# Mixing stage: output norm in the next step's first slots, decay scans behind the third low product, another spread of the logits

## What is computed

```python
def rwkv7_time_mix(z, shift0, wkv0, mu, w0, w2, a0, a2, g2, k_k, k_a, r_k, lnx_g, lnx_b):
    zm = zf + (prev - zf) * mu                      # r, k, v, xw, xa, xg are columns of zm
    wlog = -softplus(-(w0 + tanh(xw) @ w2)) - 0.5
    decay = exp(-exp(wlog))
    a = sigmoid(a0 + xa @ a2)
    g = sigmoid(xg) @ g2
    kk = heads(k * k_k);  kk = kk * rsqrt(max(sum(kk * kk), 1e-24))
    k = k * (1.0 + (a - 1.0) * k_a)
    # per row: s = s * w + (s @ -kk) (kk * a)^T + v k^T;  y = s @ r
    y, s_new = wkv7_scan(rh, heads(decay), kh, vh, -kk, kk * ah, wkv0)
    y = (y - mean) * rsqrt(var + LN_X_EPS)          # the output norm, per head
    y = y.reshape(B, L, RWKV_DIM) * lnx_g + lnx_b
    bonus = sum(rh * kh * r_k) * vh
    return (y + bonus) * g, s_new, z[:, -1:]
# in layer_forward, of the same projection p = h @ w_in:
    gate_logits = p[..., MLA_COLS + RWKV_COLS:]     # 2048 columns
    x = x + sum(sigmoid(gate_logits) * proj)
```

## Time and profile before

| | us |
|---|---|
| median of the timed runs (3) | 1544.85 |
| lowest, highest | 1543.92, 1545.82 |
| the profiled execution | 1542.08 |
| its span, first to last instruction | 1540.3 |
| PE busy in the span | 1440.2 (94%) |
| DVE busy | 854.1 (55%) |
| ACT busy, POOL busy | 474.3, 153.9 |
| mean granted clock of PE, share of full speed | 0.976 |

### The profile page before, as it was taken

How to read it: one execution, slowest core, us unless ns; L and a number is a source line. 1 busy time by engine, 2 the same in 40 slices (tenths; PEclk the granted TensorE clock), 3 DMA queues, 4 the chain that set the end, 5 groups by cost and what they waited for, 6 DMA issues and landing times. The chain is left out here.

```text
span 1540.3 us, 39034 instructions
## 1 busy us (share of the span) xinstructions
PE 1440.2 (94%) x16352; PEld 1001.3 (65%) x16352; DVE 854.1 (55%) x1942; ACT 474.3 (31%) x986; POOL 153.9 (10%) x145
## 2 busy tenths in 40 slices
PE   6999999999899999999998899979998799999994
PEld 5888888875465665566554566644554677777772
DVE  3555555565767887788775666646777123222220
ACT  2222222225334434433421344434553111111110
POOL 0000000000001011101111000000000222333321
PEclk9999999999999999999998999989999899999998
DMA  9522221446232223222114533437955999999962
GB/s 336 200 96 95 95 95 68 144 160 211 63 113 85 86 85 116 74 67 72 50 55 112 126 88 87 109 119 296 347 194 184 315 330 342 343 354 356 346 237 43
DMA packets 101937, 257.62 MB, mean 167 GB/s; under 512 B 35360, under 2 KB 54448, under 8 KB 92432
## 3 DMA queue, kind: packets, MB, share of 16 engines
q1 hardware_dynamic: 94032, 237.95, 45.0%
q0 software_dynamic: 7744, 17.33, 4.8%
HBM read 203.36 MB, written 60.56 MB: 171 GB/s over the span
## 5 line engine op out<-in xcount | busy, mean ns | idle before, releaser
L559 PEld LDWEIGHTS a_ps<-a_hT,a_wz 128*128 128x128 f32 x1792 | 202.6, 192 | 6.1 <-issue 3.8
L559 PE MATMUL a_ps<-a_hT,a_wz 128*128 128x128 f32 x1792 | 204.1, 275 | 1.7 <-DMA a_wz<-w_z 1.7
L2080 PE MATMUL d_ps<-late,last_down 128*128 128x512 f32 x256 | 115.1, 596 | 1.7 <-DVE last_down L1828 1.0
L2461 DVE TENSOR_SCALAR f_y<-f_down,table 96x512 f32<-96x512 f32 x32 | 23.9, 747 | 119.3 <-PE f_down L2255 73.6
L2262 DVE COPY f_xT<-f_turned 128x384 f32<-128x384 f32 x32 | 17.8, 558 | 125.1 <-PE f_turned L2229 122.5
L2080 PEld LDWEIGHTS d_ps<-late,last_down 128*128 128x128 f32 x256 | 46.6, 190 | 51.1 <-issue 49.7
L1586 ACT ACTIVATE late<-c_score,c_top 128x1024 f32<-128x1024 f32 (+8 forms) x72 | 50.5, 702 | 92.3 <-DVE c_top L1535 91.8
L1222 PE MATMUL b_ps<-b_wg,r_hT 128*128 128x512 f32 x128 | 65.8, 637 | 0.4 <-DMA r_hT<-hT_d 0.4
L2468 ACT ACTIVATE f_xT<-f_turned 128x384 f32<-128x384 f32 x32 | 15.7, 490 | 162.7 <-PE f_turned L2229 159.3
L1008 DVE STREAM_TRANSPOSE b_U<-b_T 64x256 f32<-64x256 f32 x144 | 63.3, 439 | 2.7
L906 DVE TENSOR_TENSOR b_M<-b_ps,r_causal 128x512 f32<-128x512 f32 x72 | 46.3, 685 | 32.8 <-PE b_ps L1285 32.8
(11 more groups left out here) (381 smaller groups left out, 2831.1 us busy)
## 6 DMA issues: line engine op xcount, KB each, us to landing
wgu<-w_gate_up SPq DMA_DIRECT2D x15, 2048.0 KB
late<-w_gate_up SPq DMA_DIRECT2D x9, 2048.0 KB
wd<-w_down SPq DMA_DIRECT2D x17, 1024.0 KB
late<-w_down SPq DMA_DIRECT2D x10, 1024.0 KB
r_hT<-hT_d SPq DMA_DIRECT2D x16, 512.0 KB, 4.3
b_hT<-hT_d SPq DMA_DIRECT2D x16, 512.0 KB, 3.9
gate_d<-b_logits SPq DMA_DIRECT2D x32, 256.0 KB, 4.1
late<-gate_d SPq DMA_DIRECT2D x8, 1024.0 KB, 6.6
```

The costliest lines, as they stand in the source:

```text
L559: mm = pe.matmul(banks[Z_BANKS[n % 2]][:, j * P:(j + 1) * P], wz[:, i, (g + j) * P:(g + j + 1) * P], hT[t % 2][:, i, :], start=(i == 0), s ...
L2080: mm = pe.matmul(banks[2 + u][:], oT[t % 2][:, HB * branch(u) + k, :], wo[:, HB * branch(u) + k, half(u)], start=(k == 0), stop=(k == HB - 1))
```

## The change

1. `FILL_STEADY` spreads the same 25 slices of a step otherwise: none in slots 2 and 4, six in slot 5. In slot 0 one of the three slices comes behind the low product.
2. `centred` and `variance` of a tile move from slot 8 to slots 0 and 1 of the next step, `root` (ACT) from slot 11 to slot 2 of the next step, behind `copy_w`, and `finish` from slot 1 to slot 4. The last tile keeps its places.
3. `decays` moves from slot 3 to slot 4, and so behind the copy of the third low product; `finish` and then `keys` follow.
4. SP stores the output in slot 5, and takes up items slot by slot, no more once a step.

```diff
--- before.py
+++ after.py
@@ -713,7 +713,7 @@
 
         unit_of, tile_of = lambda q: q // NT, lambda q: q % NT
         FILL_FIRST = (3,) * NL + (2,) * NL
-        FILL_STEADY = (2, 2, 2, 2, 3, 2, 2, 4, 2, 1, 1, 2)
+        FILL_STEADY = (3, 2, 0, 3, 0, 6, 2, 4, 1, 1, 1, 2)
         FILL_TAIL = (2, 2, 2, 2, 2, 2, 2, 2, 1, 1, 1, 1)
         FILL_END = (1, 0, 0, 2, 0, 1, 4, 0, 0, 0, 0, 0)
         full_of = lambda q: q - unit_of(q)
@@ -724,7 +724,7 @@
         parts_upto = lambda q: (q // NT * NT - q // NT + q % NT) * DC + q // NT * 2
 
         BEGUN = 6
-        fill_upto = lambda s: BEGUN + sum(fill_of(i, k) for i in range(-1, s + 1) for k in range(2 * NL))
+        fill_upto = lambda s, k: BEGUN + sum(fill_of(i, j) for i in range(-1, s + 1) for j in range(2 * NL if i < s else k + 1))
         stores_upto = lambda q: 16 * sum(1 if tile_of(i) < LAST else len(QUADS) for i in range(q % 2, q, 2))
 
         def fill_of(s, k):
@@ -775,15 +775,15 @@
             sp.dma_start(hT_tail[:], io["hT_d"][LAST][:, :, 0:DEC]).then_inc(tail_in, 16)
             q = 2
             for s in range(-1, NT + 1):
-                if s >= 2:
-                    sp.wait_ge(out_ready, s - 1)
-                    sp.dma_start(io["ob_d"][s - 2], y[:]).then_inc(ob_stored, 16)
-                for item in range(6):
-                    if s == LAST and item == 2:
+                for k in range(2 * NL):
+                    if s >= 2 and k == 5:
+                        sp.wait_ge(out_ready, s - 1)
+                        sp.dma_start(io["ob_d"][s - 2], y[:]).then_inc(ob_stored, 16)
+                    if s == LAST and k == 7:
                         sp.wait_ge(bon_done, NT)
                         sp.wait_ge(v_turned, NT)
                         load_head(sp, io, early, 0, 0, early["head_in0"])
-                    if q < ITEMS and parts_upto(q + 1) <= fill_upto(s):
+                    while q < ITEMS and parts_upto(q + 1) <= fill_upto(s, k):
                         if tile_of(q) < LAST:
                             load_hT(full_of(q) + 2)
                         elif unit_of(q) + 2 < UNITS:
@@ -1014,7 +1014,7 @@
                 for k in range(2 * NL):
                     if there(s) and k // 2 < levels_of(s):
                         (low, merge)[k % 2](s, k // 2)
-                    if there(t) and k == 8:
+                    if t == LAST and k == 8:
                         centred(t)
                         variance(t)
                     if there(n):
@@ -1022,18 +1022,23 @@
                             keys_squared(n)
                         if k == 2:
                             sums(n)
-                        if k == 3:
+                        if k == 4:
                             decays(n)
-                        if k == 4:
-                            keys(n)
                         if k == 6:
                             scaled_inverse(n)
                         if k == 7:
                             scaled_ar(n)
                         if k >= 8:
                             products(n, k - 8)
-                    if k == 1 and there(t - 1):
-                        finish(t - 1)
+                    if there(t - 1):
+                        if k == 0:
+                            centred(t - 1)
+                        if k == 1:
+                            variance(t - 1)
+                        if k == 4:
+                            finish(t - 1)
+                    if there(n) and k == 4:
+                        keys(n)
                     if there(t):
                         if k == 5:
                             next_state(t)
@@ -1195,7 +1200,9 @@
                             last_low(s)
                         if k == 11:
                             last_merge(s)
-                    if there(t) and k == 11:
+                    if there(t - 1) and k == 2:
+                        root(t - 1)
+                    if t == LAST and k == 11:
                         root(t)
 
         @block.tensor
@@ -1394,11 +1401,13 @@
                     if k == 0:
                         if there(t):
                             right_side(t)
-                        fill(fill_of(s, k))
+                        fill(fill_of(s, k) - 1 if solving else fill_of(s, k))
                     if solving:
                         (low, merge)[k % 2](s, k // 2)
                     if k > 0:
                         fill(fill_of(s, k))
+                    elif solving:
+                        fill(1)
                     if there(t):
                         if k == 2:
                             solved(t)
```

## The result

| | before | after |
|---|---|---|
| median of the timed runs, us | 1544.38 | 1558.66 (1556.09 to 1562.13, 4 runs) |
| profiled execution / its span, us | 1542.08 / 1540.3 | 1556.09 / 1554.3 |
| first low product of step 0 | 390.19 | 390.66 |
| first low product of step 8 | 793.21 | 801.42 |
| first score product of attention | 842.90 | 852.43 |

The changed kernel is slower: ratio 1.0092, 95% interval 1.0073 to 1.011, some 14 us. The forecast had slower by 3.5 us, with a range up to 1554: the direction was right, the size was not. The ratios here leave out three timed runs of one kernel ("GpSimd quiet", 1564 to 1568 us), which lay over 1.5% above its fastest.

The account below looks back on a forecast made before the run. TensorE's queue was taken to set each mixing step (busy 48.5 of 49.8 us). Terms gave +5.9 us without the clock, then -6.9 and +4.5 for the clock: +3.5 on the 1544.85 median, 1548.4 us; range 1538.5 to 1554.

Parts of the forecast that it names:

- steps 2 to 7, full clock: Mixing steps 2 to 7 take 50.1 us instead of 49.8 through a wait before the bonus factors: +1.8 in all.
- step 6, its own wait: In step 6 PE waits 3.3 us once for ScalarE's logits copy, queued behind the gate's copy: +2.4 net.
- end of the stage: Tile 7's root stands behind the copy of W, so its output is stored later, delaying the last y copy: +1.1.
- clock losses at step starts: Four low-clock losses behind the two waits at step starts vanish once a slice fills the second wait: -6.9 us.
- new clock losses: Low clock after new waits: 1.3 for step 6's 3.3 us wait, 1.6 each in two of five other steps: +4.5.
- The new wait: Before the bonus factors (L1279), PE waits about 1.0 to 1.1 us for DVE's L896 in steps 2 to 7.
- Rival 1: The sum holds, but the wait before the bonus factors is too short to lower the clock: 1545 us; chance 0.25.
- rival 2: DVE's run is shorter than summed, so no wait before the bonus factors; steps of 49.0, 1538 us; chance 0.16.
- rival 4: The first merge still waits because centring on DVE holds up the merge's addition; worth 0; chance 0.05.
- rival 3: The wait before the bonus factors brings the lower clock in every step: +8.6, or 1554 us with GpSimd's share; chance 0.14.
- the run on DVE (20.41): DVE's unbroken work from the third low product's copy to L896's end grows from 17.55 to 20.41 us.
- 30%: Possible slowdown of three two-input DVE instructions beside GpSimd, instead of 7%: 0.6 a step, another 4 us, outside the sum.

Follow-up runs that it names:

- GpSimd quiet: The changed kernel with GpSimd's three products on the output replaced by one of 8 columns; median 1549.7 us, ratio 1.0033 to the kernel before.
- second profile: The changed kernel itself, unedited, profiled and timed once more; median 1564.2 us, ratio 1.0120 to the kernel before.
- best kernel: The changed kernel with scans ahead of the third low copy, gate copy behind the logits copy, last two tiles' norm at old places; 1531.7 us, ratio 0.9929.

## Why the prediction was right in direction and wrong in size

The sum was made against the profile. To the first score product it can be checked term by term:

| term | predicted | profile | second profile |
|---|---|---|---|
| start of step 0 (the stage ahead) | 0 | +0.5 | +2.0 |
| step 0 | +1.1 | +1.0 | +1.0 |
| step 1 | -0.5 | -0.7 | -0.7 |
| steps 2 to 7, full clock | +1.8 | +5.2 | +5.2 |
| step 6, its own wait | +2.4 | +2.2 | +2.2 |
| end of the stage | +1.1 | +1.3 | +1.3 |
| clock losses at step starts | -6.9 | -7.3 | -7.3 |
| new clock losses | +4.5 | +7.3 | +16.7 |
| sum | +3.5 | +9.5 | +20.4 |
| stages behind | 0 | +4.5 | +1.5 |

(Step 6: 3.29 less the 1.12 that the other steps have. New losses: 4.7 + 2.6 in the first profile, 4.7 + 6.3 + 3.1 + 2.6 in the second. Losses at step starts: 7.3 is all that steps 1 to 7 have above 49.79 before, with 0.2 in step 3, which lost no clock. Stages behind: from the first score product to the end of the span 697.4 before, 701.9 and 698.9 after.) Against the forecast the first profile is 10.5 us too long: 3.4 from the steps at full clock, 2.8 from the new clock losses, 4.5 from the stages behind. The second is 18.5 too long, 12.2 of it from the new clock losses.

**Right.** PE's own 49.0 us were shown by two kernels (48.98). The new wait stands where it was put, before L1279, behind L896. Step 0, step 1, the end and the place and size of step 6's wait (3.29 for 3.3) came within 0.3 us each. (Step 0 has a bonus wait of 0.71 besides, which the prediction did not have; it is hidden in the sum of the step, but in the second profile it cost 4.7 us of clock.) The first merge no longer waits, and the losses of clock at the starts of the full steps are gone. Rival 1 (the wait is too short for the clock) fails on step 4, rival 2 (no new wait, 1538) and rival 4 on the timeline, and rival 3 (low clock in every step) on the steps that kept it, four of five in the first profile. The best kernel shows, though, that rival 2's price, 49.0 a step, was there to be had.

**Right by luck: the size of the wait.** It measured 1.12 us for "1.0 to 1.1", but neither end of it is where the sum had it. DVE released the bonus factors 33.96 us after the first low product, for 33.42; PE came there at 32.84, for 32.40. The two errors cancel in the wait. They do not cancel in the step, which follows DVE: 33.96 + 16.70 = 50.66, for 50.1.

**Wrong: the run on DVE (20.41).** It measured 20.91, from the copy at 602.29 to L896's end at 623.20, and this 0.50 is nearly all of what the step has more than forecast. The failed step is the one on GpSimd beside DVE: "0.15 a step, 1 us in all, inside my rounding". The sum had nothing for it. L879 alone costs 0.67 a step (the run is 0.50 longer and not 0.67, because the sum had the rest of it 0.17 too long). The row it rested on was misread: the earlier trace rows shows L936 at 0.74, but L936 began at 828.86 and L835 ended at 827.78 + 1.26 = 829.04. They lay side by side for 0.18 us. That is no price for overlap, it is the tail of one. What had to be asked is when, in the new order, a product of GpSimd will be under way as a two-input instruction starts. The prediction gave GpSimd's products 16.4 to 20.4 after the first low product, and L879 follows the scans, `finish` and the reciprocal, at 19.6 (608.86). The collision could have been read from the sum's own times. That L936 and L940, also named, would be free of it in a full step could be read there too: they come at 24.0 and 24.7, and GpSimd, its bonus products included, stops at 23.2. In the last two steps, which are shorter, they do collide: L936 takes 1.77 and 1.37 there, instead of 0.69 and 0.74, and L940 1.65 in the last, instead of 0.69. The 4 us that the prediction set apart for "30%" on three instructions is about what 97% on one of them cost (0.67 in six steps); that the two agree is luck. The kernel with GpSimd quiet, in which the collision is gone and step 6's wait with it, has a step of 49.99, near the 50.1 of the sum.

PE's being 0.4 us late at the bonus factors (part of it because `values` now waits for L940) adds nothing to the step, since DVE comes later still.

**Wrong: what a wait costs in clock.** "Two of the other five as costing 1.6 each" took its price from the old losses, where the low clock lasted 3.4 us. Behind the new wait it lasted 10.2 us in step 4 of the first profile (at 622 to 634 the mean clock is 0.58) and 6.8 to 13.7 us in the three profiles with this DVE run, and cost 3.1 to 6.3 us. The "two of the other five" had no row behind it; that it is near what was found (one and two of these five in the two profiles, 8 of 19 in three) is luck. The upper bound of 9.6 was too low: the second profile has 16.7. This is the second failed step, and in the second profile the larger one: the price of a wait, 1.6, was taken over from another place. So the end of the range, 1554, was built on a bound that the trace of before could not give, since no row there had a wait of this length at this place.

**The stages behind** moved by +4.5 in the first profile, and nothing ties this to the change: in its second profile it was +1.5. Over the thirteen profiles here, all of kernels whose edits end before attention, that stretch lasted 697.4 to 704.8 us; the kernel before, with 697.4, is the shortest of them, and the one with the single slice moved in it has 700.0. The experts' products wait 6.2 us in all for their weights after, and 2.5 before. What sets this from run to run stays open.

So the whole is this: the new table, the split and the norm's move are worth about 0.8 us a step and 7 us of clock, and the best kernel gets both. The scans behind the third copy, together with `finish` and GpSimd's products, take it back: they make the DVE run 3.4 us longer (17.55 to 20.91 us), 1.1 more than PE covers, and the wait that comes of it is followed, in nearly half of the cases, by a long stretch at the lower clock.

## What to carry to other kernels

Before an instruction chain with two SBUF inputs is moved, lay GpSimd's intervals over it at the new times. What counts is not the overlap in per cent but which GpSimd instruction is under way at each start. A price for contention may only be read from a row in which the two lie side by side for their whole length. And where the engine that sets the time is to be covered, count the cover ahead of each of its waits: a slice moved from ahead of one wait to ahead of the next made one long wait out of two short ones, and one slice in the right place was worth 15 us here.

## What the runs showed of the hardware

- A DVE instruction that reads two tiles in SBUF and a GpSimd product that reads SBUF take turns: L879 0.69 alone and 1.36 beside L843; L874 0.69 alone and 1.58 beside L835; four scans of 128 columns 1.37, 2.51 and 4.28 us beside none, two and four products. The one that came second lost some 0.14 us less than what was left of the other (0.67 of 0.81, 0.33 of 0.47, and 1.08 of 1.22 for L936 in step 8 of the changed kernel). GpSimd's own product was lengthened where it came second to a product of 512 columns (L834 1.37 instead of 1.04), and kept its 1.26 or 1.04 beside the scans. In the last step of the changed kernel L945, a product with a constant that reads one tile in SBUF, took 1.15 beside L834 instead of 0.43.
- A wait of 0.7 to 1.1 us on PE, followed by products of few columns, was followed by a fall of TensorE's clock from 2.4 to 1.2 GHz in 8 of 19 cases, for a loss of 3.1 to 6.3 us each. Where PE waited 0.3 us or less there, with one slice or two ahead, it never happened (67 steps). A wait of 3.3 us in step 6 cost 2.6 on top of itself in both profiles of the changed kernel; one of 2.43 at the same place, in the kernel with a slice at the bonus factors, cost no clock.
